# Seven-product pairs of a two-layer decoder kernel: two loads of 512 KB per pair in place of four of 256 KB

## The reference, cut to what matters

```python
def swiglu(x, w_in, w_out):
    a, b = jnp.split(x @ w_in, 2, axis=-1)      # w_in: 1024 x 5632, D_FF = 2816
    return (jax.nn.silu(a) * b) @ w_out

for l in range(DEPTH):                           # DEPTH = 2
    h = h + 0.5 * swiglu(rmsnorm(h, ffn1_norm[l]), ffn1_w_in[l], ffn1_w_out[l])
    ...                                          # mixer
    h = h + 0.5 * swiglu(rmsnorm(h, ffn2_norm[l]), ffn2_w_in[l], ffn2_w_out[l])
return rmsnorm(h, final_norm)
```

## Time and profile before

| | |
|---|---|
| runs | 2169.77, 2169.83, 2170.68 us |
| median | 2169.83 us |
| the profiled execution | 2170.19 us, its span 2168.4 us |
| PE | busy 2132.7 us (98%) |
| DVE | 1374.6 us (63%) |
| ACT | 879.5 us (41%) |
| POOL | 1382.0 us (64%) |
| mean granted clock of TensorE | 0.996 of full speed |
| bytes read | 206.48 MB, 97 GB/s over the span |

### The profile page before, as it was taken

One profiled execution on the slowest core, in us unless ns is written; L12 is line 12 of the kernel. 1 busy time (PEld: TensorE's weight loads), 2 busy tenths in 40 slices (PEclk: granted clock), 3 DMA queues, 4 the chain that ended last, 5 costly groups with the idle time before them and its releaser, 6 DMA issues.

```text
span 2168.4 us, 36196 instructions
## 1 busy us (share of the span) xinstructions
PE 2132.7 (98%) x12838; PEld 1880.6 (87%) x12838; DVE 1374.6 (63%) x2598; ACT 879.5 (41%) x1733; POOL 1382.0 (64%) x1030
## 2 busy tenths in 40 slices
PE   8999999999999999999999999999999999999997
PEld 6998998878888789899879889988888887998996
DVE  6762886478755477177568548746887455762863
ACT  4531542444553254054145235325445533531541
POOL 5775777644446657677667767785444374776773
PEclk9999999999999999999999999999999999999999
DMA  4342333322213223333323433332222132232332
GB/s 170 98 155 91 112 95 121 102 68 64 74 54 103 97 82 102 100 103 98 102 89 108 153 101 103 94 126 87 64 74 68 49 118 78 98 105 90 117 95 81
DMA packets 90028, 210.81 MB, mean 97 GB/s; under 512 B 9824, under 2 KB 13064, under 8 KB 89608
## 3 DMA queue, kind: packets, MB, share of 16 engines
q1 hardware_dynamic: 85680, 203.32, 29.1%
q10 hardware_dynamic: 4184, 5.31, 0.7%
HBM read 206.48 MB, written 3.68 MB: 97 GB/s over the span
## 4 chain that ended last, share of the span: by engine, by line
PE 87%; DVE 7%; ACT 3%; issue 2%; DMA 1%; ACTq 0%; POOL 0%; DVEq 0%; POOLq 0%
PE bank L865 16%; PE bank L866 15%; PE bank L867 15%; PE bank L1001 11%; PE bank L1003 11%; PE bank L1002 11%; PE tbank L1217 1%; DVE mem L2034 1%; DVE bank L2009 1%; ACT u1H L1547 1%; DVE ssq L2017 1%; DVE h L2014 1%; PE obank L1263 0%; DVE yL L2042 0%; DVE bank L2024 0%
## 5 line engine op out<-in xcount | busy, mean ns | idle before, releaser
L737 POOL TENSOR_TENSOR wL<-raw,wH 128x1024 fp32r<-128x1024 f32 (+3 forms) x280 | 549.5, 1962 | 23.3
L734 POOL TENSOR_SCALAR wH<-raw 128x1024 fp32r<-128x1024 f32 (+3 forms) x280 | 248.2, 886 | 489.3 <-PE bank L867 424.8
L1001 PE MATMUL bank<-u1H,wH 128*128 128x256 f32 x1152 | 326.4, 283 | 3.0 <-DVE hidL L1936 3.0
L1002 PE MATMUL bank<-u1H,wL 128*128 128x256 f32 x1152 | 326.0, 283 | 0.0
L1003 PE MATMUL bank<-u1L,wH 128*128 128x256 f32 x1152 | 326.0, 283 | 0.0
L865 PE MATMUL bank<-u1H,wH 128*128 128x512 f32 x704 | 281.5, 400 | 0.0
L866 PE MATMUL bank<-u1H,wL 128*128 128x512 f32 x704 | 275.0, 391 | 0.0
L867 PE MATMUL bank<-u1L,wH 128*128 128x512 f32 x704 | 274.8, 390 | 0.0
L865 PE MATMUL bank<-hidH,wH 128*128 128x512 f32 x704 | 274.4, 390 | 0.0
L866 PE MATMUL bank<-hidH,wL 128*128 128x512 f32 x704 | 274.0, 389 | 0.0
L867 PE MATMUL bank<-hidL,wH 128*128 128x512 f32 x704 | 273.9, 389 | 0.0
(11 more groups left out here) (295 smaller groups left out, 4737.7 us busy)
## 6 DMA issues: line engine op xcount, KB each, us to landing
raw<-in_wA SPq DMA_DIRECT2D x296, 256.0 KB, 3.1
raw<-in_wM SPq DMA_DIRECT2D x96, 512.0 KB, 3.3
raw<-in_wB SPq DMA_DIRECT2D x64, 384.0 KB, 3.1
raw<-in_wB SPq DMA_DIRECT2D x64, 320.0 KB, 2.9
raw<-in_wA SPq DMA_DIRECT2D x28, 512.0 KB, 3.3
raw<-in_wR SPq DMA_DIRECT2D x32, 256.0 KB, 2.6
mem<-in_memT SPq DMA_DIRECT2D x2, 1024.0 KB, 8.1
near_bias<-bias_rows ACTq DMA_DIRECT2D x2, 1024.0 KB, 6.0
```

The lines of the kernel that those rows point to most:

```text
L734: pool.tensor_scalar(wH[:, w, 0:cols], raw[:, slot, 0:cols], 1.0, 0.0, ALU.mult, ALU.add).then_inc(rounded, 1)
L737: pool.tensor_tensor(wL[:, w, 0:cols], raw[:, slot, 0:cols], wH[:, w, 0:cols].bitcast(F32), ALU.subtract).then_inc(split_done, 1)
L1001: pe.matmul(dst, a, hi, start=begin and k == 0, stop=False)
L1002: pe.matmul(dst, b, hi, start=False, stop=False)
```

## The change

For K pairs the four quarter loads become two loads of a whole row each, 128 x 1024 numbers, 512 KB. The first goes when both A11 and A12 of the pair before are free, the second when both A21 and A22 are. Two semaphores, one for each row, take the place of four, and all who waited for a quarter wait for its row. Nothing is changed on PE, and no instruction of POOL, ACT or DVE is added, removed or moved.

```diff
-        quarter_landed = {n: sem("quarter_" + n) for n in ("A11", "A21", "A22", "A12")}
+        row_landed = [sem(f"row_landed{s}") for s in range(RAW_SLOTS)]
...
-                        for q in ("A11", "A12", "A21", "A22"):
-                            s, half = int(q[1]) - 1, int(q[2]) - 1
+                        for s, (q, r) in enumerate((("A11", "A12"), ("A21", "A22"))):
                             if p.run == 0:
                                 sp.wait_ge(split_done, l * UNITS + u_first[f] + p.unit - 2 + s + 1 + RAW_SLOTS)
                             else:
                                 quarters_free(q, g - 1)
-                            sp.dma_start(quarter(q), wA[src + s, :, half * 4 * P:half * 4 * P + 4 * P]
-                                         ).then_inc(quarter_landed[q], 16)
+                                quarters_free(r, g - 1)
+                            sp.dma_start(raw[:, s, :], wA[src + s, :, :]).then_inc(row_landed[s], 16)
...
-                    pool.wait_ge(quarter_landed["A11"], 16 * (g + 1))
-                    pool.wait_ge(quarter_landed["A21"], 16 * (g + 1))
+                    pool.wait_ge(row_landed[0], 16 * (g + 1))
+                    pool.wait_ge(row_landed[1], 16 * (g + 1))
...
-                    pool.wait_ge(quarter_landed["A22"], 16 * (g + 1))
+                    pool.wait_ge(row_landed[1], 16 * (g + 1))
...
-                        act.wait_ge(quarter_landed["A22"], 16 * (g + 1))
+                        act.wait_ge(row_landed[1], 16 * (g + 1))
...
-                        act.wait_ge(quarter_landed[name], 16 * (g + 1))
+                        act.wait_ge(row_landed[int(name[1]) - 1], 16 * (g + 1))
...
-                        dve.wait_ge(quarter_landed["A12"], 16 * (g + 1))
+                        dve.wait_ge(row_landed[0], 16 * (g + 1))
```

## The result

| | before | after |
|---|---|---|
| median of 16 runs each | 2169.56 us | 2174.84 us |
| lowest, highest | 2168.22, 2171.90 | 2171.78, 2177.53 |
| ratio of the medians | | 1.0024, 95% interval 1.0018 to 1.0031 |
| profiled execution (span) | 2170.19 (2168.4) | 2171.78 (2170.0) |

The change costs 5.3 us. In two later comparisons the same kernel took 2176.3 us against 2169.4 of before, ratios 1.0032 (1.0022 to 1.0043) and 1.0031 (1.0021 to 1.0042), so 5 to 7 us is the size. The first profile of the changed kernel happens to be its quickest execution of all; its span is only 1.6 us over before. It shows where the loop stands and hardly what it costs; for the cost I use two further traces.

What follows compares the result with a forecast made beforehand. PE was taken as the bound, busy 10.08 us of each 10.08 us pair. Issues 0, POOL 0, late landings +0.5 and entries +0.6 gave +1.1 on 2169.83, so 2171 us, range 2169 to 2178.

Steps and rivals of the forecast that it cites:

- first entry: First entry from standard pairs into seven-product pairs, where PE waits 1.1 us: -0.4 to +1.6 us, taken as 0.
- signs of being wrong: In the seven-product pairs: periods over 10.08 us, ACT's A11 rounding waiting for a DMA, PE waiting for DVE's L1888.
- Fewer loads are worth nothing: In 72 seven-product pairs, 288 loads become 144; the issue time saved, about 0.33 us each, is worth 0.
- The loop of the first row: A11 rounding to next A11 rounding, through sigmoid, DVE, issue and landing: 9.86 us, below PE's 10.08, so PE stays bound.
- The landing of the first row: A11 and A12's joint 512 KB load lands 3.4 us after issue, between bounds of 3.3 and 4.6.
- Late landings: Over 56 looped periods, about one landing in twelve a us late: 0.5 us lost; single landings matter over 4.95 us.
- the start of part 1: Entry from output units into part 1's seven-product pairs: no PE wait there, and a us later costs 0.
- The other three entries: Part 0's entries after its first: steps PE waits for come 0.2 us later, 3 x 0.2 = 0.6 us.
- The second row and POOL: A21 and A22's load lands at 96.3, POOL starts some 1.3 us later, hidden by slack; cost to PE 0.
- Rival 1: Both rows slow each other; first lands in 3.9 to 4.6 us, ACT's wait sets the period, up to 2214; chance 0.13.
- Rival 3: POOL's sums plus second-row issue and landing pass 10.08 us if that row takes 4.8 or more; 2208; chance 0.03.
- rival 2: PE's 3.0 us of waits at the four entries into seven-product pairs vanish, 2167 us at best; chance 0.03.

Runs made afterwards that it cites:

- the third trace: The changed kernel run a third time without any edit, for one more trace: 2176.32 us, ratio 1.0031 against the kernel before.
- the dose: Against the changed kernel, the two loads of a pair swapped so the second row goes first: 2232.74 us, ratio 1.0300 to the kernel before.

## Why the prediction was right, and where it was not

The measured 2174.84 lies in the range of 2169 to 2178, but 3.8 us over the 2171 that I gave as the likeliest, and its loss of 0.24% is just past the 0.2% within which I had put 83% of the chance. The forecast loss was 1.1 us, the measured one 5.3. That the range holds it is partly luck: its upper part was there for first rows that land after 3.9 us, and the time came from other things, one slow landing at the first entry and the start of the long runs. All three signs of being wrong that I had named turned up in some pairs: periods over 10.08, A11's rounding waiting for a DMA, and PE waiting for L1888.

- **Fewer loads are worth nothing.** Right. The loads fell to half and the rest of the program did not move.
- **The loop of the first row.** Right in its parts: I had 6.28 us to the release and 0.08 to the issue, measured 6.36 to 6.37; the time from the landing to ACT's start is 0.02 to 0.03, not 0.1. So the break-even is 3.69, not 3.6. The slack ahead of PE, put at 1.35, is 1.39. That PE and the loop stand within tenths of each other was the point of the prediction and is what the traces show. The run with ACT's wait moved shows that the loss goes by way of what stands behind that wait.
- **The landing of the first row** is the term that was mis-sized. I took 3.4 (3.3 of a lone load, and 0.1 for a load behind it). The medians are 3.5 to 3.6, the means up to 3.66, where the earlier trace rows gave 3.3 and the 0.1. I had asked only what a 256 KB load suffers from one behind it; the first row has 512 KB of its own time in which a second load is issued. Against 0.2 us made good per pair an error of 0.1 to 0.2 is most or all of it.
- **Late landings.** Forecast 0.5 us, measured 2 to 4 in part 1. A single landing was to cost something only from 4.95 us on; at the second pair of a long run one of 4.16 cost 1.1 us. The step that failed is the start of part 1, which I had put at 0 ("a us later costs 0"): the long run begins with no more than 0.5 of the 1.39 us of slack.
- **The first entry.** I gave -0.4 to +1.6 and took 0. In two of three traces the first row there landed after 5.1 to 5.3 us, and the run took 3 us more. The row at the third trace's entry:

```profile
67.87 0.39 PE L1000 MATMUL bank<-u1H,wH 128*128 128x256 f32 x1 [2.48 <-DVE hidL L1935]
```

  Against 1.1 before. In the kernel before a slow A12 (4.8 us) holds up one step of ACT there; a slow row holds up all. I had allowed it to be slow again at a cost of 1.6 and took 0; the cost was 3. In the first trace the row took 4.0 there and 0.3 was lost. The other three entries cost 0.1 to 0.2 each, as forecast.
- **The second row and POOL.** Right in the middle of a run: POOL starts 1.3 us later, its wait ahead of the second sum is gone, PE never waits for its remainders, and the second row alone costs nothing. The two rows together land 4.9 us after the first is issued. Wrong at the start of the long runs, where "nothing of this reaches PE" does not hold: I had priced only POOL's remainders and its own circle, not the wait of SP for POOL's low part of A12. That wait holds back the first row by up to 0.95 us there, and it set the pace when I delayed the second row.
- **Rival 1** (the rows slow each other, the loop sets the period) held in a mild form: late by tenths, not by a us. At the dose of 4.3 us its rule gives 4 x (6 x 0.6 - 1.35) + 4 x (8 x 0.6 - 1.35) = 23 us, and 64 were measured; it is a lower bound, since entries and slow landings count in full too. **Rival 3** (POOL's own circle) and **rival 2** (gains at the entries) did not come.

## What to carry to other kernels

Where a transfer lies in a loop with the engines (buffer free, issue, landing, use, buffer free), add up the loop and compare it with the period of the engine that bounds: if the slack is no more than the spread of the landings, a change that looks free can cost some of it. Do it for every semaphore that the load waits for, and at the start of a run as well as in its middle: here the middle of a run could have 1.39 us in hand and the start had next to none. Joining loads moves the first use to the landing of the whole and the issue to the end of the last reader; each may be harmless where both are not. The cheaper remedy may be the order of the instructions behind the wait: put what the loop needs ahead of it.

## What was not expected of the hardware

Two loads of 512 KB issued 0.43 us apart land 1.24 us apart, the first after 3.7 and the second after 4.5 us (shown above, in the first trace of the changed kernel). Issued 1.19 us apart, as in the run with the second row first, they land 2.1 apart: the first after 3.3, the later one after 4.2 from its own issue. The issues at 251.4 and 252.6:

```profile
L676 SPq DMA_DIRECT2D raw<-in_wA x1: 332/332/332, 251.4 to 251.4; - x1
...
DMA to landing us min/median/max: 3.3/3.3/3.3
...
L676 SPq DMA_DIRECT2D raw<-in_wA x1: 328/328/328, 252.6 to 252.6; - x1
...
DMA to landing us min/median/max: 4.2/4.2/4.2
```

In the 64 pairs of this trace in which the order is swapped the later load took 3.8 to 6.0 us, median 4.4. So in these two examples a load issued while another was under way took 0.8 to 0.9 us longer than the one ahead of it, whether it came 0.43 or 1.19 us behind; why, no run here shows.

Slow landings are not all chance. The row that was slow (4.2 to 4.3 us) at the third pair of the run of 928 us was so in all three traces of the changed kernel, and the one for the fourth pair of the short run before it took 4.4, 4.2 and 4.2, against medians of 3.5 to 3.6. What slows them, no run here shows.
